# A running sum of score tiles kept in place, and the first gate tiles moved into the last attention step

## The reference, cut to what matters

```python
proj = xn @ w_in
y_a    = a_b * causal_depthwise_conv(a_c * a_x, conv_a_w)        # branch 0
y_sb   = stick_breaking_attention(q, k, v)                       # branch 1, 4 heads
y_fox  = forgetting_attention(q, k, v, dcum)                     # branch 2, 4 heads
y_conf = silu(layer_norm(conv31(u * sigmoid(u_gate))))           # branch 3
for g in range(4):
    gate = sigmoid(xn @ w_gate[g] + b_gate[g])
    h = h + gate * (branches[g] @ w_branch[g])
x = x + h @ w_out
x = x + hierarchical_moe(rms_norm(x), ...)

# stick-breaking attention, per head
log_not = where(mask, log_sigmoid(-z), 0)
after = cumsum(log_not, axis=3, reverse=True) - log_not          # sum over all later keys
w = where(mask, exp(log_sigmoid(z) + after), 0)
```

## Time and profile before

| | us |
|---|---|
| Median of 3 runs | 769.8 |
| Lowest and highest | 769.7 and 771.23 |
| The profiled execution's own time | 778.17 |
| Its span, from first to last instruction | 775.8 |
| TensorE busy | 714.3 (92%) |
| VectorE busy | 342.0 (44%) |
| ScalarE busy | 246.0 (32%) |
| GpSimd busy | 84.1 (11%) |

### The profile page before, as it was taken

The page is one execution under the profiler, slowest core; times in us unless marked ns, Lnnn a source line. Parts: engine busy times, 40 slices in busy tenths (PEclk is TensorE's granted clock), DMA queues, the critical chain, the costliest instruction groups (busy, mean ns, idle before and its releaser), DMA issues.

```text
span 775.8 us, 9657 instructions
## 1 busy us (share of the span) xinstructions
PE 714.3 (92%) x3887; PEld 524.4 (68%) x3887; DVE 342.0 (44%) x635; ACT 246.0 (32%) x397; POOL 84.1 (11%) x128
## 2 busy tenths in 40 slices
PE   4999799999999999799999999699999998878785
PEld 4887788877777777488888888575555554545442
DVE  5378974245555656545454403723221121112146
ACT  7222124466656556532333311211011111001014
POOL 3002902000000000000002000011211111111000
PEclk9999899999999999889999999879999999999898
DMA  6522323220122222193222598679999999999972
GB/s 222 161 67 97 109 63 123 80 68 27 45 68 67 68 69 68 35 317 112 91 68 107 225 422 306 242 258 400 414 416 420 421 417 419 418 420 418 419 307 112
DMA packets 61567, 166.59 MB, mean 215 GB/s; under 512 B 8069, under 2 KB 39890, under 8 KB 49101
## 3 DMA queue, kind: packets, MB, share of 16 engines
q1 hardware_dynamic: 55884, 153.86, 52.1%
q0 software_dynamic: 5632, 12.05, 4.1%
HBM read 158.31 MB, written 15.99 MB: 225 GB/s over the span
## 4 chain that ended last, share of the span: by engine, by line
PE 77%; DMA 9%; SPq 6%; DVE 5%; ACT 2%; issue 1%; POOL 0%; POOLq 0%; DVEq 0%; ACTq 0%
PE psum L1513 29%; PE psum L1612 12%; PE psum L1860 10%; PE psum L1772 6%; PE psum L1899 5%; SPq L438 5%; DMA ring_p<-in_w_expert_up 4%; PE psum L1624 3%; DMA ring_h<-in_w_expert_down 2%; PE psum L1650 2%; DVE sg L976 1%; PE psum L1680 1%; PE psum L1678 1%; DMA raw<-in_w_in 1%; DMA y_dram<-ye,slots 1%
## 5 line engine op out<-in xcount | busy, mean ns | idle before, releaser
L1513 PE MATMUL psum<-xh,wh 128*128 128x512 f32 x272 | 108.1, 397 | 5.6 <-DVE xl L976 2.9
L1513 PE MATMUL psum<-xl,wh 128*128 128x512 f32 x272 | 107.6, 396 | 0.0
L1513 PE MATMUL psum<-xh,wl 128*128 128x512 f32 x272 | 107.5, 395 | 0.0
L979 DVE TENSOR_TENSOR wl<-raw,wh 128x1280 fp32r<-128x1280 f32 (+4 forms) x37 | 71.8, 1945 | 51.7 <-ACT wh L689 22.0
L976 DVE SCALAR_TENSOR_TENSOR hid<-psum,rslot,act_g 128x256 f32<-128x256 f32 x17 | 8.2, 484 | 126.0 <-ACT act_g L930 126.0
L1513 PEld LDWEIGHTS psum<-xh,wh 128*128 128x128 f32 x272 | 52.0, 191 | 16.9 <-DVE xl L976 3.1
L1513 PEld LDWEIGHTS psum<-xh,wl 128*128 128x128 f32 x272 | 52.1, 191 | 11.0
L1513 PEld LDWEIGHTS psum<-xl,wh 128*128 128x128 f32 x272 | 52.1, 192 | 10.9
L930 ACT ACTIVATE act_g<-psum,rslot 128x256 f32<-128x256 f32 x17 | 8.1, 474 | 160.6 <-PE psum L1860 160.6
L1612 PE MATMUL psum<-xh,wh 128*128 128x512 f32 x128 | 52.6, 411 | 0.0
L1612 PE MATMUL psum<-xl,wh 128*128 128x512 f32 x128 | 51.8, 405 | 0.0
(11 more groups left out here) (319 smaller groups left out, 1450.6 us busy)
## 6 DMA issues: line engine op xcount, KB each, us to landing
raw<-in_w_gate SPq DMA_DIRECT2D x16, 1024.0 KB, 6.4
raw<-in_w_in SPq DMA_DIRECT2D x10, 1024.0 KB, 5.6
ring_w<-in_w_expert_up SPq DMA_DIRECT2D x9, 1024.0 KB, 29.1
ring_w<-in_w_expert_down SPq DMA_DIRECT2D x8, 1024.0 KB, 18.4
ring_h<-in_w_expert_gate SPq DMA_DIRECT2D x8, 1024.0 KB, 24.5
ring_e<-in_w_expert_gate SPq DMA_DIRECT2D x8, 1024.0 KB, 29.0
ring_h<-in_w_expert_down SPq DMA_DIRECT2D x7, 1024.0 KB, 13.2
ring_e<-in_w_expert_down SPq DMA_DIRECT2D x7, 1024.0 KB, 16.7
```

Source lines behind the costliest of these rows:

```text
L979: return dve.tensor_tensor(dst, src, hi.bitcast(F32), ALU.subtract)
L1513: last = nc.tensor.matmul(dst, a, b, start=start and n == 0, stop=stop and n == len(seq) - 1)
```

## The change

In the loop, GpSimd now adds, after it has masked the weights of a step with `kt` 2 or 1, the tile `sp[kt + 1]` to `sp[kt]` in the columns that both have (128 or 256 columns). `sp[kt + 1]` then holds the sum over all later tiles, and TensorE needs a single `neg_one` product for it. GpSimd waits for `acc_done` of the step before it adds. The semaphore `sp_mask` becomes `sp_made`, which counts the masks and the sums: the step with `kt` 1 or 0 waits for both.

The generator `x_products` gets two more tiles at its end: the gate tiles of the first unit of branch 1, written into banks 6 and 7. Ten matmuls each are taken three times in step 15, the last 18 of 48 by `gates(2*3*KC)` behind the loop. The gate stage leaves these two out, and their sigmoid reads banks 6 and 7.

```diff
+        def sp_made(n):
+            h, i = divmod(n, NT)
+            return h * (2 * NT - 2) + max(2 * i, 1)
...
                 pool.wait_ge(S["w_exp"], n + 1)
                 select(None, P, ALU.is_gt, 0.0, 0, 1, -1, view=wts[:, q0:q0 + P]).then_inc(S["w_mask"], 1)
+                if 0 < kt < NT - 1:
+                    pool.wait_ge(S["acc_done"], n + 1)
+                    pool.tensor_tensor(sp[:, kt, q0 + P:], sp[:, kt, q0 + P:], sp[:, kt + 1, q0 + P:], ALU.add).then_inc(S["sp_made"], 1)
...
-                    act.activation(gs[:, m, :], bank[m][:, :], ACT.Sigmoid,
+                    act.activation(gs[:, m, :], bank[m if g > 1 or cg else 6 + m][:, :], ACT.Sigmoid,
...
+                for m in range(2):
+                    s = GATE0 % 2
+                    f = slice(m * P, (m + 1) * P)
+                    gate_w = [w[:, s, 0:KC * UC].rearrange("p (c n) -> p c n", c=KC) for w in (wh, wl)]
+                    pe.wait_ge(S["split_ready"], GATE0 + NX + 1)
+                    pe.wait_ge(S["xg_neg"], STEPS - 1 + m)
+                    for c in range(KC):
+                        for q, (a, b) in enumerate(((gate_w[0], xh), (gate_w[0], xl), (gate_w[1], xh))):
+                            last = nc.tensor.matmul(bank[6 + m][:, :], a[:, c, f], b[:, c, :], start=c == 0 and q == 0, stop=c == KC - 1 and q == 2)
+                            if c == KC - 1 and q == 2:
+                                last.then_inc(S["gate_ps"], 1)
                             yield
...
-                    pe.wait_ge(S["sp_mask"], n + 1)
+                    pe.wait_ge(S["sp_made"], sp_made(n))
                     last = nc.tensor.matmul(bank[0][:, q0:], neg_tri[:, :], sp[:, kt, q0:], start=False, stop=True, skip_group_check=True)
-                    for k2 in range(kt + 1, NT):
-                        last = nc.tensor.matmul(bank[0][:, k2 * P:], neg_one[:, :], sp[:, k2, k2 * P:], start=False, stop=True, skip_group_check=True)
+                    if kt < NT - 1:
+                        last = nc.tensor.matmul(bank[0][:, q0 + P:], neg_one[:, :], sp[:, kt + 1, q0 + P:], start=False, stop=True, skip_group_check=True)
...
             pe.sem_inc(S["br_ps"], BR0)
+            gates(2 * 3 * KC)
...
-                        pe.wait_ge(S["gate_free"], d + (1 - KC))
-                        passes(bank[m][:, :], [(gate_w[0][:, c, f], gate_w[1][:, c, f], xh[:, c, :], xl[:, c, :])
-                                               for c in range(KC)]).then_inc(S["gate_ps"], 1)
+                        if g > 1 or cg:
+                            pe.wait_ge(S["gate_free"], d + (1 - KC))
+                            passes(bank[m][:, :], [(gate_w[0][:, c, f], gate_w[1][:, c, f], xh[:, c, :], xl[:, c, :])
+                                                   for c in range(KC)]).then_inc(S["gate_ps"], 1)
```

More of the change, by code:

```diff
@@ L280, in hybrid_trunk @@
             "fbc_ready dc_psum dc_out dq_psum dq_out "
-            "z_psum sp_min sp_ln sp_max sp_mask acc_done w_exp w_mask o_hi o_split wv_done "
+            "z_psum sp_min sp_ln sp_max sp_made acc_done w_exp w_mask o_hi o_split wv_done "
             "l_psum l_max l_bias l_exp l_norm pt_psum pt_out fo_psum fo_hi fo_split "
@@ L599, in _ @@
                 pool.wait_ge(S["sp_max"], n + 1)
-                select(None, P, ALU.is_gt, 0.0, 0, 1, -1, view=sp[:, kt, q0:q0 + P]).then_inc(S["sp_mask"], 1)
+                select(None, P, ALU.is_gt, 0.0, 0, 1, -1, view=sp[:, kt, q0:q0 + P]).then_inc(S["sp_made"], 1)
                 pool.wait_ge(S["w_exp"], n + 1)
                 select(None, P, ALU.is_gt, 0.0, 0, 1, -1, view=wts[:, q0:q0 + P]).then_inc(S["w_mask"], 1)
+                if 0 < kt < NT - 1:
+                    pool.wait_ge(S["acc_done"], n + 1)
+                    pool.tensor_tensor(sp[:, kt, q0 + P:], sp[:, kt, q0 + P:], sp[:, kt + 1, q0 + P:], ALU.add).then_inc(S["sp_made"], 1)
             pool.wait_ge(S["fo_psum"], STEPS)
@@ L1627, in x_products @@
                             yield
+                for m in range(2):
[9 more added lines that the diff above has]
+                                last.then_inc(S["gate_ps"], 1)
+                            yield
             products = x_products()
```

## The result

The changed kernel takes 764.83 us (median of 11 runs, 762.07 to 768.19) beside 773.48 us for the kernel before (11 runs, 769.7 to 777.36): a ratio of 0.990, 95% interval 0.9878 to 0.9922. The forecast was 761.2 us with a range of 758.3 to 764.2, that is 8.6 us off a base of 769.8. The base was 773.48. The medians differ by 8.65 us; the ratio, which is not that of the two medians, gives 7.7 us, with 6.0 to 9.4 in its interval. So the direction came as forecast and the size within the interval, and the time lies 0.6 us above the range.

What follows compares the result with a forecast made beforehand. TensorE was taken as the limit, busy 92% of the span. Loop 2.8 plus gate stage 5.9 gave 8.7 us off the profiled 778.17, scaled by 0.989 to 8.6 off 769.8: 761.2 us, own range 759.8 to 762.8, held range 758.3 to 764.2.

Steps and rivals of the forecast that it cites:

- The running sum: Attention loop, steps 0 to 14: fewer `neg_one` products on TensorE save 2.8 us; the added GpSimd sums cost 0.
- the cover: GpSimd in the loop: the sum has 5.6 us to spare ahead of the next mask, 8.1 us ahead of TensorE.
- a collision: GpSimd and VectorE share SBUF interfaces, so two-input instructions clash; in the loop 1.7 us at most, hidden, costing 0.
- The fill: Step 15 into the gate stage: gate matmuls put TensorE 10.5 us ahead; the third unit starts 5.9 us sooner.
- Both waits: Gate stage: TensorE stands 2.1 us before the second unit and up to 2.45 us before the third.
- The 5.9 us: Gate stage: third unit's start gained against the earlier profile, where it began at 358.63, and kept by later units.
- rival 1: Gate stage: the clock falls behind the second wait, costing 1.7 to 2.6 us; gain 6.5, 763.3 us; chance 20%.
- called covered: Gate stage: a clock fall behind the first wait costs nothing, as TensorE has 2.45 us to spare at the third unit.
- The base: Whole kernel: unprofiled time before the change taken as 769.8 us, the median of the runs shown, with 8.6 us off.
- Rival 2: Gate stage: third unit's weights land early, leaving only the wait before the second unit; gain 11.2, 758.7 us; chance 12%.

Runs made afterwards that it cites:

- the sixteen fills: Changed kernel with sixteen counting fills of a 128x512 tile on GpSimd ahead of each of the eight sums: 792.75 us, ratio to before 1.0248.
- eight fills: Changed kernel with eight counting fills of a 128x512 tile on GpSimd ahead of each of the eight sums: 767.88 us, ratio to before 0.9938.
- the pair of orders: Changed kernel with third unit's weights loaded ahead of output weights, and first unit's sigmoid and sum ahead of the first output-weight share: 760.06 us, ratio to before 0.9839.
- the load alone: Changed kernel with only SP's order turned round, third unit's weights loaded ahead of the eight output-weight transfers: 765.26 us, ratio to before 0.9886.
- the sigmoid alone: Changed kernel with only ScalarE's and VectorE's order turned round, first unit's sigmoid and sum ahead of the first output-weight share: 768.12 us, ratio to before 0.9923.
- the fill alone: Kernel before with only step 15 filled with gate tiles, the `neg_one` products left as they were: 772.04 us, ratio to before 0.9981.
- The sum alone: Kernel before with only GpSimd's running sum and the single `neg_one` product, last step and gate stage unchanged: 769.54 us, ratio to before 0.996.

## Why the prediction was right, and where it was not

**The running sum: right.** 2.8 us forecast, 2.83 measured in every profile that has it (but for the sixteen fills). The sum on GpSimd takes 0.46 us for 128 columns and 0.74 for 256, where 0.8 was taken for the larger, and TensorE never waits for it. Of the cover, eight fills reached 5.8 us without a price, and sixteen showed what lies behind it: eight waits, up to 3.3 us. One reading under it was wrong: that the two durations in the earlier trace rows, 1.40 and 3.41 us beside VectorE's convolution, agree with a collision. These are VectorE's rows in the profile before at the two places:

```profile
77.32 11.56 DVE L976 SCALAR_TENSOR_TENSOR sg<-cu,ch,sg 128x512 f32<-128x512 f32 x10
...
89.28 2.28 DVE L979 TENSOR_TENSOR wl<-raw,wh 128x2048 fp32r<-128x2048 f32 x1
```

The 1.40 us at 78.92 are beside the convolution, whose instructions read two tiles in SBUF as well, and they are about what the sums of 0.46 and 0.74 us give for 512 columns (an estimate: 1.3). The 3.41 us at 89.29 are beside the split of a weight tile. So only the second bears a collision out. The sum in the loop is clear of both, since VectorE is idle beside it.

**The fill: right to 0.3 us up to the third unit.** From step 15's scores to the second unit 21.23 us were forecast and 21.43 and 21.24 measured; to the third 37.3, and 37.61 and 37.34 measured. Both waits are there, with the releaser forecast, VectorE's product. Their causes are shown by the pair of orders: turned round together they take both waits away, the load alone takes the second, and the sigmoid alone the first.

**The comparison with before: about 0.8 us too much.** The 5.9 us of the forecast were taken from a profile in which the clock stood low for 5.2 us behind 328.84. In the second profile of the same program the third unit starts at 42.42 instead of 43.21. Against that one the fill is worth 4.8 and 5.1 us up to the third unit, in the two profiles of the changed kernel.

**The clock: rival 1 holds in some executions.** It had 20 in 100. Five profiled executions have both waits, and each shows a fall behind just one of them. In three it is the second (the changed kernel's first, the fill alone, the sixteen fills), which is rival 1. In two it is the first (the changed kernel's second, the eight fills), which the forecast called covered, and so it was: their second wait is 0.63 and 0.70 us. Forecast and rival exclude each other in one execution, as rival 1 says, but the kernel does both. Up to the projection the gain is 8.6 us at the most (273.70 less 265.08 from the loop's start) and 5.9 at the least (272.91 less 266.97). The timed ratios of 0.990 and 0.9887 are 7.7 and 8.8 us.

**The base: the step that failed.** The prediction's sum ended with "The median of the runs shown is 769.8, 0.989 of it, so 8.6 us off". This took three runs within 1.5 us of each other for the kernel's time. They are the low end of a wide spread: 64 later runs of before gave medians of 772.28 to 775.54 and lie between 769.17 and 776.55 us, and the base of the result, these three runs and eight more, was 773.48. The range held only what was unknown of the change and nothing of the base, and its 1.5 us for what a measurement can tell is less than the 6 to 7 us over which one program spreads. Rival 2 reasoned from the same gap: "the runs without the profiler are 1% shorter". Against 773.48 the 778.17 of the profiled execution is 0.6% longer, and all twelve profiled executions lie above the median of their own runs, by 0.2 to 4.7 us. So a part of the gap goes with the profiled execution and a part was the low base. With 773.48 the same 8.6 us give 764.9, and 764.83 was measured. That this fits to 0.1 us is luck: the ratios say 7.7 and 8.8, each with 1.7 to 2.5 us either way, and of the terms the 5.9 was too high against one profile of before and the clock's cost, which it left out, came in three profiled executions of five. That the spread comes largely from the clock after waits elsewhere in the kernel is supported by the stage ahead of the loop (0.99 and 0.95 of full clock, 5.9 us apart) and by the correlation of -0.78; that nothing else adds to it isn't shown.

**Not settled.** The sum alone and the fill alone were timed at 3.1 and 1.5 us, together 4.6, and the change at 7.7. The difference of 3.1 is slightly more than the three intervals allow together (2.8), so that they simply add up is doubtful. In the profiles, each against the second of before and up to the projection, it is 2.55 and 2.42 us, and 5.94 for both, 0.97 more. Of this 0.69 is the longer step 15 of the fill alone (the third unit at 38.30 instead of 37.61): the two `neg_one` products of step 15 count in full only where the fill keeps TensorE from waiting. The other 0.28 is the last step of the sum alone, 42.70 us to the third unit against 42.42. Where the remaining 2 us of the timed runs come from stays open.

## What to carry to other kernels

When an engine at the limit gets filler for its waits, work out what now stands behind it in the orders of the other engines and queues: here 10.5 us of head start left 5 to 6, since a load and a sigmoid stood behind work that nobody needed yet, and turning both orders round brought the third unit another 4.4 to 4.6 us forward (ratio 0.9839). Turn them together, since a single one made the remaining wait longer or uncovered the fall of the clock. And before a time is forecast, and not a difference, ask how far runs of one program lie apart: three that agree don't tell it.

## What the runs showed of the hardware

- Standing for 2.0 to 2.3 us sometimes brings TensorE's clock down to 1.2 GHz and sometimes does not, in one and the same program: at the first wait it fell after 2.02 us in one profile and stayed after 2.21 in the other. After 4.25 us it fell for longer. A fall after 2.0 to 2.6 us cost 1.6 to 1.8 us (83.30 against 81.68 us from the third unit to the projection; 15.35 against 13.6 for one unit), the one after 4.25 us 2.7 (84.32).
- A fall cost nothing where TensorE had a wait ahead that was longer than it; the wait then shrank by it (2.30 to 0.63 us).
- The third unit's weights, 1.25 MB behind 4 MB of output weights in one queue, landed 13.4 us after their issue (12.8 before), though the order of everything else around them had changed.
- A sum of 128x512 on GpSimd took 1.40 us beside VectorE's scalar-tensor-tensor of the convolution and 3.41 us beside its subtraction of two weight tiles (128x2048, 2.28 us).
